# The zeroing of the y banks, the routing and the job table of a two-layer trunk in a new order, and one fp32 product ahead of the branch pieces

## What is computed

```
for l in range(DEPTH):                              # DEPTH = 2
    h = rms_norm(x, g_mix[l])
    u = jnp.einsum('bsd,dc->bsc', h, w_in[l])
    y_pool = pool_mixer(...); y_conv = conv_module(...); y_attn = forgetting_attention(...)
    gates = jax.nn.sigmoid(u[..., OFF_G:] + b_gate[l]).reshape(B, S, N_BRANCH, D)
    merged = (gates[:, :, 0] * (y_pool @ w_br_pool[l]) + gates[:, :, 1] * (y_conv @ w_br_conv[l])
              + gates[:, :, 2] * (y_attn @ w_br_attn[l]))
    x = x + merged @ w_out[l]
    h = rms_norm(x, g_ffn[l])
    if l % 2 == 0:                                  # D_FF = 2816
        x = x + swiglu(h, ffn_w1[i], ffn_w3[i], ffn_w2[i])
    else:                                           # 8 experts, top 2, D_FF_EXPERT = 3584
        x = x + moe_ffn(h, router_w[i], exp_w1[i], exp_w3[i], exp_w2[i])
```

## Time and profile before

| | us |
|---|---|
| median of 3 runs | 1623.88 |
| lowest, highest | 1623.3, 1625.89 |
| the profiled execution | 1626.2 |
| its span, first to last instruction | 1624.4 |
| TensorE busy in it | 1609.7 (99%) |
| VectorE busy | 1286.4 (79%) |
| ScalarE busy | 1040.1 (64%) |

### The profile page before, as it was taken

How to read it: one execution, slowest core, us unless ns; L and a number is a source line. 1 busy time by engine, 2 the same in 40 slices (tenths; PEclk the granted TensorE clock), 3 DMA queues, 4 the chain that set the end, 5 groups by cost and what they waited for, 6 DMA issues and landing times.

```text
span 1624.4 us, 24061 instructions
## 1 busy us (share of the span) xinstructions
PE 1609.7 (99%) x9601; PEld 1417.5 (87%) x9601; DVE 1286.4 (79%) x1132; ACT 1040.1 (64%) x942; POOL 18.8 (1%) x19
## 2 busy tenths in 40 slices
PE   9999999999999999999999999999999999999998
PEld 8999999999998997888888888888888888888887
DVE  6895874545798677987987987987997987987986
ACT  6545554335545646776777777776777777677774
POOL 0000100000000010000000000000000000000000
PEclk9999999999999999999999999999999999999999
DMA  9544555555444454998998998999999999999994
GB/s 301 163 143 136 167 179 182 181 183 193 145 154 150 136 165 170 372 373 325 373 372 325 372 371 328 367 373 341 363 364 342 363 362 345 363 361 343 362 362 178
DMA packets 182455, 452.61 MB, mean 279 GB/s; under 512 B 7168, under 2 KB 81024, under 8 KB 182272
## 3 DMA queue, kind: packets, MB, share of 16 engines
q1 hardware_dynamic: 182400, 451.82, 77.4%
HBM read 450.74 MB, written 1.05 MB: 278 GB/s over the span
## 4 chain that ended last, share of the span: by engine, by line
PE 93%; DVE 4%; ACT 1%; DMA 1%; SPq 0%; issue 0%; DVEq 0%; ACTq 0%
PE bank L300 28%; PE bank L302 28%; PE bank L301 28%; PE bank L1579 2%; DVE w_low L290 2%; PE bank L1600 2%; PE bank L1621 1%; DMA raw<-w_in 1%; PE bank L1229 0%; PE bank L1390 0%; PE bank L1406 0%; PE bank L1338 0%; PE bank L1389 0%; PE bank L1397 0%; ACT w_high L286 0%
## 5 line engine op out<-in xcount | busy, mean ns | idle before, releaser
L290 DVE TENSOR_TENSOR w_low<-raw,w_high 128x2048 fp32r<-128x2048 f32 x426 | 955.3, 2287 | 120.8 <-ACT w_high L286 120.5
L286 ACT ACTIVATE w_high<-raw 128x2048 fp32r<-128x2048 f32 x426 | 801.3, 1917 | 142.7 <-DMA raw<-exp_w 138.8
L300 PE MATMUL bank<-w_high,hg_high 128*128 128x512 f32 x896 | 352.3, 393 | 2.5 <-DVE w_low L290 2.5
L302 PE MATMUL bank<-w_high,hg_low 128*128 128x512 f32 x896 | 349.7, 390 | 0.0
L301 PE MATMUL bank<-w_low,hg_high 128*128 128x512 f32 x896 | 349.6, 390 | 0.0
L300 PE MATMUL bank<-h_high,w_high 128*128 128x256 f32 x1024 | 290.9, 284 | 0.0
L302 PE MATMUL bank<-h_high,w_low 128*128 128x256 f32 x1024 | 285.5, 279 | 0.0
L301 PE MATMUL bank<-h_low,w_high 128*128 128x256 f32 x1024 | 285.5, 279 | 0.0
L300 PEld LDWEIGHTS bank<-w_high,hg_high 128*128 128x128 f32 x896 | 168.7, 188 | 37.9 <-DVE w_low L290 2.9
L302 PEld LDWEIGHTS bank<-w_high,hg_low 128*128 128x128 f32 x896 | 168.6, 188 | 35.6
L301 PEld LDWEIGHTS bank<-w_low,hg_high 128*128 128x128 f32 x896 | 168.6, 188 | 33.9
(11 more groups left out here) (282 smaller groups left out, 1593.0 us busy)
## 6 DMA issues: line engine op xcount, KB each, us to landing
raw<-exp_w SPq DMA_DIRECT2D x336, 1024.0 KB, 5.1
raw<-w_in SPq DMA_DIRECT2D x41, 1024.0 KB, 5.1
raw<-ffn_w SPq DMA_DIRECT2D x33, 1024.0 KB, 5.2
raw<-w_out SPq DMA_DIRECT2D x8, 1024.0 KB, 5.1
raw<-w_br_attn SPq DMA_DIRECT2D x4, 1024.0 KB, 5.1
raw<-w_br_pool SPq DMA_DIRECT2D x2, 1024.0 KB, 4.8
raw<-w_br_conv SPq DMA_DIRECT2D x2, 1024.0 KB, 4.8
cst<-consts SPq DMA_DIRECT2D x1, 1280.0 KB, 13.7
```

The costliest lines, as they stand in the source:

```text
L286: nc.scalar.activation(wh[c % RING][:], raw[c % RING][:], ACT.Copy).then_inc(s["high_done"], 1)
L290: nc.vector.tensor_tensor(wl[c % RING][:], raw[c % RING][:], wh[c % RING][:].bitcast(F32), ALU.subtract).then_inc(s["split_done"], 1)
L300: pe.matmul(dst, lh, rh, start=start and i == 0, stop=False)
L302: last = pe.matmul(dst, ll, rh, start=False, stop=stop and i == len(terms) - 1)
```

## The change

- **The y banks.** The first two dense pieces put their two halves crosswise into banks 0 and 2 (before: banks 0, 6 and 2), so banks 4 to 7 are free and are zeroed inside the first piece, behind its sixth of eight channel groups. The zero tile's memset moves ahead on DVE. The wait for `d_scaled` goes; `block_steps(first=True)` waits for both pieces and multiplies in two halves.
- **norm_stats of layer 0** moves one piece later: the first two quarters behind out pieces 27 and 28, the last two behind the zeroing. The last out unit writes bank 1, not 5.
- **Routing.** On TensorE the last token sums stand ahead of the last logits, six keep-awake matmuls stand ahead of the counts, the turns of x behind them and, for two, behind the gathers; gathers go 0, 2, 1, 3, and job 0 starts when two are copied out. ACT loads the square-root table ahead of its last squares, and Silu's table ahead of job 0.
- **The job table** is cut in two: `job_weights` (7 instructions) stands in job 0 behind the first round, its Exp on ACT with two table loads behind the same round; `job_extras` (32 instructions) stands behind piece 116.
- **One fp32 product**, `ones` by 256 columns of constants into bank 3, ahead of the branch pieces of both layers. Nothing reads it.

```diff
-UNIT_BANK = [0, 1, 2, 4, 5, 0, 1, 2, 4] + [u % 3 for u in range(9, UNITS - 1)] + [5]
+UNIT_BANK = [0, 1, 2, 4, 5, 0, 1, 2, 4] + [u % 3 for u in range(9, UNITS - 1)] + [1]
...
-GATHER_BANKS = (0, 5, 1, 6)
+GATHER_ORDER = (0, 2, 1, 3)
+GATHER_BANKS = (0, 1, 5, 6)
...
                         if m < 3:
                             split_high(act, MOE0 + m)
+                        if m == 2:
+                            root_table()
...
-                for g in range(4):
+                for g in GATHER_ORDER:
                     gather_out(g, 0)
-                act.wait_ge(s["r_lg"], 1)
-                nc.scalar.activation(wt[:, 1, :], wt[:, 0, :], ACT.Exp).then_inc(s["r_exp"], 1)
+                x_out(2)
+                x_out(3)
+                nc.scalar.activation(root2[:, 0:1], warm, ACT.Silu)
...
                         for a in range(2):
                             silu(j * JOB_PIECES + (c + 4), a)
+                        if isinstance(j, int) and i == 0:
+                            act.wait_ge(s["r_lg"], 1)
+                            nc.scalar.activation(wt[:, 1, :], wt[:, 0, :], ACT.Exp).then_inc(s["r_exp"], 1)
+                            nc.scalar.activation(root2[:, 0:1], warm, ACT.Silu)
...
                     if first:
                         both = rinv[:, 0:S].unsqueeze(1).to_broadcast([P, 2, S])
-                        dve.wait_ge(s["used"], DENSE0 + 1)
-                        for m, b in enumerate((0, 6)):
+                        dve.wait_ge(s["used"], DENSE0 + 2)
+                        for m, b in enumerate((0, 2)):
...
-                job_table()
-                stepped()
-                dve.wait_ge(s["x_copied"], 4)
...
                         if i:
                             split_low(dve, c + 10, r0)
+                        if isinstance(j, int) and i == 0:
+                            job_weights()
...
                         if i:
                             split_low(dve, c + 11, r0)
+                        if isinstance(j, int) and i == 1:
+                            job_extras()
+                            stepped()
                         c += 12 if i else 10
...
+                pe.matmul(bank[3][:, S:2 * S], ones[:], C(C_IDENT, 2), start=True, stop=True)
                 u = 21
...
-                    if n > P_OUT and l == 0:
-                        norm_stats(1, n - P_OUT - 1)
+                    if n > P_OUT + 1 and l == 0:
+                        norm_stats(1, n - P_OUT - 2)
...
                         if ahead and 6 in ks:
+                            pe.wait_ge(s["zeros"], 1)
+                            for m in range(4):
+                                zero_bank(4 + m)
+                            norm_stats(1, 2)
                             norm_stats(1, 3)
...
-                        if first and u == 0:
-                            pe.wait_ge(s["zeros"], 1)
-                            pe.wait_ge(s["d_scaled"], 2)
-                            for m in range(4):
-                                zero_bank(4 + m)
...
                     r0, c = j * EXP_BLOCKS, MOE0
-                    pe.wait_ge(s["m_gout"], j * 4 + 4)
-                    c = up(c, r0, (0,), 4)
+                    pe.wait_ge(s["m_gout"], j * 4 + 2)
+                    c = up(c, r0, (0,), 4, j * 4 + 4)
                     c = up(c, r0, (1,), 4)
+                    if isinstance(j, int):
+                        pe.wait_ge(s["x_copied"], 4)
```

More of the change, by code:

```diff
@@ L948, in mixer @@
                 for m in range(4):
+                    if l == 0 and m == 2:
+                        nc.vector.memset(zero[:].bitcast(F32), 0.0).then_inc(s["zeros"], 1)
                     residual(33 + m)
@@ L1076, in job_table, with job_extras @@
                 stepped()
+            def job_extras():
+                iota8 = C(C_IOTA)[:, 0:8]
                 step(nc.vector.tensor_scalar(cnt[:, 1, :], cnt[:, 0, :], P + 0.5, None, ALU.is_gt))
@@ L1503, in up @@
                                     pe.wait_ge(s["h_low_done"], 4 + k // 2 + 1)
-                                ins = products(pe, bank[6 if ahead and m else b][:, m * S:m * S + S], [
+                                at = (1 - m if c == DENSE0 + 1 else m) * S
+                                ins = products(pe, bank[(0, 2)[m] if c in (DENSE0, DENSE0 + 1) else b][:, at:at + S], [
                                     (H[:, k, m * P:m * P + P], L[:, k, m * P:m * P + P], H_in[:, k, :], L_in[:, k, :])],
@@ L1524, in dense, with pair @@
                 up(DENSE0 + 1, 0, 2, yH, yL)
-                def pair(i, first=False):
+                def pair(i):
                     for u in range(2):
@@ L1546, in experts @@
                 token_sums(2)
-                keep_awake(5, 1, *still)
+                keep_awake(2, 5, *still)
+                token_sums(3).then_inc(s["norm_stats"], 1)
                 logits(6)
                 logits(7).then_inc(s["f_raw"], 1)
-                token_sums(3).then_inc(s["norm_stats"], 1)
+                pe.wait_ge(s["xg_full"], 4)
+                turn_group(xgf, XG_BANKS[2], 2, "xg_turned")
                 small_turn(7, 0, 3, "r_logits")
-                pe.wait_ge(s["xg_full"], 4)
-                for f in range(2, 4):
-                    turn_group(xgf, XG_BANKS[f], f, "xg_turned")
-                    keep_awake(3, 5, *still)
-                pe.wait_ge(s["norm_root"], 4)
-                for f in range(2):
-                    turn_group(xT, X_BANKS[f], f, "x_turned")
-                    keep_awake(2, 5, *still)
+                turn_group(xgf, XG_BANKS[3], 3, "xg_turned")
+                keep_awake(6, 5, *still)
                 pe.wait_ge(s["r_pick"], 1)
@@ L1566, in experts @@
                 pe.matmul(bank[7][:, 64:72], C(C_ONES), sel[1], start=False, stop=True).then_inc(s["r_rank"], 1)
-                pe.wait_ge(s["ht_low"], 1)
-                turn_group(xT, X_BANKS[2], 2, "x_turned")
-                keep_awake(2, 5, *still)
-                pe.wait_ge(s["x_copied"], 1)
-                turn_group(xT, X_BANKS[3], 3, "x_turned")
+                pe.wait_ge(s["norm_root"], 4)
+                for f in range(2):
+                    turn_group(xT, X_BANKS[f], f, "x_turned")
+                    keep_awake(1, 5, *still)
                 def gather(g):
@@ L1581, in gather, with up @@
                     ins.then_inc(s["m_gather"], 1)
-                def up(c, r, banks, kn):
+                def up(c, r, banks, kn, gathered=None):
                     for k0 in range(0, KC, kn):
+                        if gathered is not None and k0:
+                            pe.wait_ge(s["m_gout"], gathered)
                         H, L = take_piece(pe, c, r, kn)
@@ L1626, in experts @@
                 pe.wait_ge(s["m_perm"], 2)
-                for g in range(4):
-                    if g:
-                        pe.wait_ge(s["ht_low"], g + 1)
+                for g in GATHER_ORDER:
+                    pe.wait_ge(s["ht_low"], (2, 3, 2, 4)[g])
                     if g == 3:
@@ L1632, in experts @@
                     gather(g)
-                pe.wait_ge(s["x_copied"], 4)
-                keep_awake(4, AWAKE_BANK, *still)
+                for f in range(2, 4):
+                    if f == 3:
+                        pe.wait_ge(s["x_copied"], 1)
+                    pe.wait_ge(s["ht_low"], 1)
+                    turn_group(xT, X_BANKS[f], f, "x_turned")
                 def job(j):
                     r0, c = j * EXP_BLOCKS, MOE0
-                    pe.wait_ge(s["m_gout"], j * 4 + 4)
-                    c = up(c, r0, (0,), 4)
+                    pe.wait_ge(s["m_gout"], j * 4 + 2)
+                    c = up(c, r0, (0,), 4, j * 4 + 4)
                     c = up(c, r0, (1,), 4)
+                    if isinstance(j, int):
+                        pe.wait_ge(s["x_copied"], 4)
                     pe.wait_ge(s["m_yhigh"], j * 2 + 2)
```

21 lines of the change are left out of this document (12 added, 9 removed).

## The result

The changed kernel takes **1627.38 us** (median of 17 runs, 1625.47 to 1630.58); the kernel before took 1624.25 us on the same chip (17 runs, 1623.29 to 1627.67). The ratio is 1.0015, 95% interval 1.0009 to 1.0022. The forecast was 1617.7 us with a range of 1614.0 to 1625.2. The measured time lies above the range, and the kernel became slower, by 0.15%, where it was to become faster. The profiled execution took 1627.38 us with a span of 1625.6, 1.2 us more than the span before.

A forecast was written before the change was run, and what follows sets the result against it. TensorE, busy for 99% of the span, was taken to bound the kernel. The terms -0.9 - 6.4 + 0 - 5.7 + 6.8 = -6.2 us, taken off with the median's offset, gave 1617.7 us, range 1614.0 to 1625.2.

The forecast's parts named there:

- The zeroing ahead of fp32 sums: Dense stage, 239 to 408 us: some 1440 products behind the new order turn from 117.7 to 113.3 ns, -6.4 us.
- The prediction's counter-argument: Layer 1's value pieces stayed slow behind norm_stats, so fp32 sums may only keep the pace they find; no gain then.
- The loss on the 156 products: Between the sums and the w2 piece, quick before: they lose 0.7 us if the pace stays slow.
- norm_stats one piece later: Ahead of layer 0's first norm_stats: TensorE's 0.87 us wait for ACT's squares goes, -0.9 us.
- The fp32 product: Ahead of both layers' branch pieces: its work mostly swallowed by the wait at piece 22; 0, bounds +1.6 and -1.3 us.
- Routing: Ahead of and in job 0: start 1.6 us earlier, piece 94's 2.48 us wait and 1.6 us of half clock gone, -5.7 us.
- The table inside job 0: Waits of 0.6, 1.1 and 3.5 us at pieces 102, 105 and 117, plus 1.6 us of half clock: +6.8 us.
- The slow dense stage: Rival: the dense stage's pace stays slow, +0.9 us, 1624.8 us, or 1623.2 if job 0's clock holds; chance 0.31.
- A chain of half clocks behind each wait in job 0: Rival: clock falls behind the 0.6 and 1.1 us waits too, dense stage slow, 1628.0 us; within the slower cases' 0.07.

The follow-up runs named there:

- g2: The kernel before with only the zeroing left out, the first w2 piece's products starting the accumulation: 1618.13 us, ratio 0.9943.
- f4: e1's kernel without the zeroing, the first w2 piece's first product into each bank starting the accumulation: 1619.07 us, ratio 0.9958.
- h2: The changed kernel with norm_stats(1, 2) moved between the halves of the first w1 piece, 18 products ahead of the zeroing and norm_stats(1, 3): 1627.51 us, ratio 1.0011.
- k1: The changed kernel without the zeroing, norm_stats(1, 2) 18 products ahead of norm_stats(1, 3), one more fp32 product behind that: 1618.47 us, ratio 0.9963.
- e1: The changed kernel with Exp in ACT's idle time and job_weights and job_extras on DVE ahead of piece 94's split: 1618.02 us, ratio 0.995.
- e2: The changed kernel with one more fp32 product of 256 columns behind the last norm_stats: 1627.53 us, ratio 1.001.
- e3: The changed kernel with two more fp32 products of 256 columns behind the last norm_stats: 1628.39 us, ratio 1.0018.
- e4: The changed kernel without the fp32 product ahead of the branch pieces of both layers: 1627.81 us, ratio 1.0011.
- g1: f4's kernel with norm_stats(1, 2) moved ahead, between the halves of the first w1 piece, 18 products between the two pairs of sums: 1617.91 us, ratio 0.9944.
- h1: e1's kernel with norm_stats(1, 2) ahead of the four zero matmuls and norm_stats(1, 3) behind them: median 1618.39 us, ratio 0.9949, in two groups.

## Why the prediction was wrong, point by point

**The zeroing ahead of fp32 sums, -6.4 us.** This is the step that failed, taken at a little under 6 in 10. Its evidence was that each of the four norm_stats ahead of layer 0's dense stage was followed by the quick pace and that four zero matmuls were followed by the slow one. Both are true, and g2 shows the second as a cause. Left out were the sums that stand in one go: four pairs at 15.96 us, in layer 0 too, with the slow pace behind them. The error was to build the new block from its parts: "sums behind it, so quick". In its place the runs showed the slow pace behind this block, in both traces of the changed kernel and in six variants of it, 117.7 ns a product, and behind two pairs of sums without any zero matmul as well (f4). The prediction's counter-argument, that sums may only keep what they find, wasn't the reason either: the block came upon the quick pace and the products behind it were slow. The change put a run of twelve records together (4 zero matmuls, 2 pairs) that had not stood in the trace before, and neither the last part (h2) nor the first (f4) decides alone. The price of the step was right: 6.4 for the pace was forecast, and k1 gives 7.5, which is 7.0 of pace over 1595 products and 0.93 of zeroing less 0.43. The loss on the 156 products that were quick before, 0.7 us, was named for this case, and came. Why this block brings the slow pace stays open.

The rule of the Trainium skill, page "TensorE: Matmul & The Clock Gate", section "Wait — 56ns, not 53.3ns?", gives columns / 2.4 GHz plus about 2.5 ns between starts at the full clock, an estimate of 109.2 ns for 256 columns, and names nothing ahead of them that would change it. No trace here shows that figure: 154 us hold 1361 or 1310 products at full clock, 113.3 or 117.7 ns, and changing the instructions ahead changed which of the two it was.

**norm_stats one piece later, -0.9.** Right: the wait is gone.

**The fp32 product, 0 within +1.6 and -1.3.** Right in its bounds. It costs 0.15 us a layer where the prediction had 0 with piece 21 quick, it does turn the 84 products quick, and behind the wait inside piece 22 either pace came.

**Routing, -5.7.** Right: -1.7 for job 0's start and -4.4 for piece 94's wait and its half clock, together -6.1.

**The table inside job 0, +6.8.** Right, with all three places. The waits were forecast as 0.6, 1.1 and 3.5 and measured as 0.62, 0.84 and 3.73; half clock fell behind the third alone. The pieces end 0.9, 1.1 and 5.3 us later, 7.4 in all, and e1 gives back 7.3.

**The rivals.** The slow dense stage was priced at 1624.8 us, 0.9 more than the kernel before. It is what happened, and on the profiled spans it is near: +1.2, with 1.0 off by chance at the start and 0.8 added by half clock in the last combine, behind a wait of 2.35 us that stood in the kernel before as well. On the medians it is 2.6 us too short. A chain of half clocks behind each wait in job 0, 1628.0, is closer to the measured time for the wrong reason: the clock stayed at 1.00 behind 0.62 and 0.84 us.

**The rest of the difference** is settled in part. The profiled spans differ by 1.2 us and the medians by 3.1, since the profiled execution of the kernel before, 1626.20 us, lay 2.0 above its kernel's median and that of the changed kernel at it. What differs between the usual executions is the granted clock. Averaged over a kernel's executions it is 0.996 in each of the six timed kernels with the table inside job 0 (the changed kernel, e2, e3, e4, h2, k1). It is 0.998 over 64 executions of the kernel before, and 0.997 to 1.000 in the timed kernels with the table ahead. A half clock of 3.4 us lowers the mean by 0.001 and costs up to 1.7 us, so 0.002 is two of them, up to 3.4 us. At one and the same mean, 0.998, four executions of the changed kernel have a median of 1626.7 us and 30 of the kernel before 1626.0, on other chips in part: 0.7 apart, near the 0.9 of the rival. So more half clock goes with the table inside job 0. The traces show one stretch behind piece 117's wait there and a second one next to it in h2 and k1; why the others come more often was not shown.

## What to carry to other kernels

Work that an engine does beside the bottleneck belongs where the engine waits anyway, not between two steps that it owes the bottleneck: the same table cost 7.3 us inside job 0 and nothing in DVE's wait ahead of piece 94. Where matmuls run back to back for hundreds of microseconds, count them per stretch: two versions, or two executions of one, may differ by 4% in pace over the same products, and here what stood ahead of them changed it, in one trace even a wait of 0.05 us. Nothing in the traces of the parts told the pace behind a block that no trace had shown: the block had to be run. And a run of sums that comes upon the slow pace can't tell whether it keeps that pace or makes it; look for one that comes upon the quick pace.

## What was not expected of the hardware

- A run of 256-column products keeps one of two paces, 113.3 or 117.7 ns, for up to 190 us, through w1, w3 and w2 pieces alike.
- A short pause can turn it (0.05 us in g1: quick to slow, 6.4 us lost) or leave it (0.06 us in h1); the times of h1's kernel lie in two groups 6 us apart, which may come from it.
- The granted clock falls to half for 3.4 us (6.8 us behind piece 117's wait in h2 and k1), and does so in some executions of a kernel and not in others: at 25 to 26 us in eight of the eighteen traces, between 603 and 613 us in eight. The largest number in one trace was four, besides the last instant.
- Leaving the zeroing of the four accumulators out, by starting the accumulation with the first product, computes the same and takes 0.93 us of TensorE away.
